# A two-layer decoder trunk: compressed-token products in four column groups of the matrix engine, a reordered way into the sparse head pairs, and the forget bias as bf16 pieces

## The chip, the core and the metric

The kernel runs on one core of a Trainium2 chip. The metric is the device time of one execution in microseconds, median of several. TensorE is called PE below, its weight loads PEld, VectorE DVE, ScalarE ACT, GpSimd POOL, and the engine that issues nearly all transfers SP.

## The reference, cut to what matters

Two layers on 256 tokens of width 2048, everything in f32. Layer 0 has 8 heads of sparse attention (compressed, selected and window branches) and 8 latent heads behind one input and one output projection. Layer 1 has 16 heads of forgetting attention. Each is followed by a SwiGLU network. Shift, scale and gate of every sub-layer come from a vector `c` through large matrices (`ada_w`, 6 x 2048 columns per layer), read whole and multiplied by `c`.

```python
def nsa_compress(k, pos_emb, w1, w2):      # blocks of 32 tokens, one every 16: 15 blocks
    blk = k[:, idx] + pos_emb[:, None, :]  # then flattened to CMP_LEN * d = 4096
    return jax.nn.silu(blk @ w1) @ w2      # w1 4096 x 256, for k and for v, two groups each
...
# forgetting attention: a bias per head, query and key on the logits
cum = lax.cumsum(jax.nn.log_sigmoid(f + f_b), axis=1)
logit = einsum(qq, k) * scale + cq[..., None] - cum[:, :, None, :]
```

## The kernel before, in words

One program per engine, with semaphores between them; nothing is scheduled at run time. The weights come through a ring of four 1 MB slots (`RAW`). SP issues the loads in one fixed order and waits, before each, until the slot four places back has been used. A slot holds one of three kinds of unit. A "w" unit is a block of a projection: ACT copies it rounded to `WHI`, DVE subtracts to get the rest `WLO` (two buffers each), and PE multiplies in three f32r products (L1129 to L1131). An "a" unit is 128 rows of `ada_w`: DVE multiplies it by a column of `c` and adds it to `ACC` (L1868 for the first, L1871 for the others), with no work for PE. An "r" unit is used by PE raw, in f32. An f32 product appears in the trace as two matmul instructions; an f32r or bf16 product as one.

**The passage to the sparse pairs.** The input projection of layer 0 runs as eight chunks, `even_in` 0 to 7; the last has 88 columns (gates and rotary key) and its result is kept as `GK`. After it come eight turns, one for each pair of sparse heads, p = 0 to 7. In a turn PE does `cmp_unit(p)` (L1411), which multiplies eight k-tiles of an r unit (`nsa_cmp_w1_k` for p below 4, `nsa_cmp_w1_v` above) by the blocks `BF` with 30 stationary columns; then `scores(p + 1)` (L1431), `values(p - 1)` (L1460 to L1463) and `turn_p(p)` (L1442, transposes of the softmaxed rows). DVE does `logits(p)` (L2159 to L2164), one a unit (L1871) and `outputs(p - 1)` (L2171 to L2184). ACT does `exps(p)` (L838) and the copy `turned(p)` (L848). SP loads one r unit and one a unit per turn.

Ahead of turn 0, DVE scales the latent rows (L2125), splits them into high and low parts (`CQH` by ACT, `CQL` by DVE, L1965), copies `GK` (L2099), does `logits(0)`, adds the four quarters of the gate vector from PE's column sums (`finish((0, G1))`, L1176 on PE and L1882 on DVE, through two PSUM banks), takes the gates from the turned `GK` (L2196, L2197), and only then builds `BF` (eight additions, L2206). `cmp_unit(0)` waits for them. ACT takes the sigmoid of the gates before `exps(0)`.

After turn 7 the sums in PSUM get their SiLU (L858), are turned (L1540), copied (L2230) and multiplied by `w2`, between the products of the latent heads.

**The forgetting attention.** Its input projection runs as 13 chunks and four more for the output gate. Eight of these 17 carry a head pair each: after their first unit PE does `fox_scores(p)`, for two heads and two row blocks: q times k in f32 (L1740), the key's forget bias (L1741, f32, 16 rows, the stationary operand a spread column of the identity that picks the head), and the causal mask (L1742, bf16). DVE turns the sums into `CUMT` once (L2608). PE turns two units later, and multiplies by the values three units later.

The causes of order are therefore the program texts of the five engines, the ring of four slots, and two buffers of `WHI`/`WLO`.

```python
def cmp_unit(n):
    ...
    ins = mm(m.PS[0:30, 0, 256 * i:256 * i + 256], m.BF[:, i, u.kt0 + k, :],
             m.RAW[:, u.s % RING, 256 * k:256 * k + 256], start=..., stop=...)
```

Of the kernel before, what the change touches and what calls it, by code (L numbers as in the profile page):

```python
# [23 lines left out]
KT = D // P  # L24
# [18 lines left out]
C_BLK, C_LEAD = 605, 609  # L43
C_ALL = 610
# [7 lines left out]
def constants():  # L52
# [14 lines left out]
    c[:, C_LEAD] = i % 32 == 0  # L67
    return c
# [122 lines left out]
class Machine:  # L191

    def __init__(self, nc, t, ctx, known):
# [20 lines left out]
        self.WLO = sb("WLO", [P, 2, 2048], F32R)  # L214

        ((self.AHI, self.ALO), (_, self.XG), (self.O, self.KN, self.RP, self.KRO, self.HCT, self.KCT, self.VCN), (_, self.BF)) = overlay(
# [3 lines left out]
             ("HCT", [P, 2, 2, 30], F32), ("KCT", [P, 32], F32), ("VCN", [P, 2, P], F32)],  # L220
            [("O_ROOM", [P, 16, T], F32), ("BF", [P, 2, 32, 30], F32)])
# [23 lines left out]
        self.NEGB = sb("NEGB", [P, P], BF16)  # L245
        self.VC = sb("VC", [P, V_ALL])
# [11 lines left out]
            [("Z", [P, 4, 2, 16], F32), ("CUM", [P, 2, 16], F32)])  # L258
# [15 lines left out]
        self.CUMT, self.FZ, self.FE, self.FL = (self.TF[0:16, i, :] for i in range(4))  # L274
        self.GK = self.TF[0:88, 0, :]
# [363 lines left out]
def scalar_program(block, nc, t, out, m):  # L639

    @block.scalar
    def _(act):
# [246 lines left out]
        hi(mla[1])  # L889
        mla_evict(0)  # L890
# [220 lines left out]
def tensor_program(block, nc, t, out, m):  # L1111

    @block.tensor
    def _(pe):
# [51 lines left out]
        def finish(v, blocks=range(KT)):  # L1166
# [3 lines left out]
            if v[1] in (G1, G2):  # L1170
                if v == (1, G1):
                    wait("t_read", ("fox", m.fox_at["k", 3]))
                for q in range(4):
# [232 lines left out]
        def cmp_unit(n):  # L1406
# [3 lines left out]
            for k in range(u.nk):  # L1410
                ins = mm(m.PS[0:30, 0, 256 * i:256 * i + 256], m.BF[:, i, u.kt0 + k, :], m.RAW[:, u.s % RING, 256 * k:256 * k + 256],  # L1411
                         start=u.kt0 + k == 0, stop=u.kt0 + k == 31)
# [123 lines left out]
        mla_unit(0)  # L1536
        for i in range(2):
            wait("st_copied", ("cmp", i))
# [4 lines left out]
        wait("t_read", ("cmp", 1))  # L1543
# [186 lines left out]
        def fox_scores(p):  # L1730
# [42 lines left out]
        def cumulate_turned():  # L1773

            wait("cum_ready", 0)
            for tb in range(2):
                ins = turn(m.PS[0:16, 5, P * tb:P * tb + P], m.CUM[:, tb, :], m.ID)
# [54 lines left out]
def vector_program(block, nc, t, out, m):  # L1832

    @block.vector
    def _(dve):
# [37 lines left out]
        def finish(v):  # L1873
# [3 lines left out]
            if seg in (G1, G2):  # L1877
                wait("grow_bias", 2 * layer + (seg == G2))
                for q in range(4):
# [113 lines left out]
        V.tensor_copy(m.IDB[:], m.ID)  # L1993
        link(V.tensor_copy(m.NEGB[:], m.CON[:, C_NEG:C_NEG + P]))
# [111 lines left out]
        def bias_masked():  # L2106
# [4 lines left out]
            link(ins)  # L2111

        def even_second(c):
# [8 lines left out]
            else:  # L2122
# [4 lines left out]
                split_lo(c.key, m.CQL[:, at:at + 4, :], m.TF[:], m.CQH[:, at:at + 4, :])  # L2127
# [88 lines left out]
        mla, mla_ada = [c.w[0] for c in m.mla_in], [[u for u in c.units if u.kind == "a"] for c in m.mla_in]  # L2216
        lo(mla[0])
# [11 lines left out]
        wait("t_done", ("cmp", 1))  # L2229
        m["t_read"].tick(V.tensor_copy(m.HCT[:].rearrange("p i j n -> p i (j n)"), m.PS[:, 6, 0:128].rearrange("p (i n) -> p i n", i=2)[:, :, 0:60]), ("cmp", 1))  # L2230
# [445 lines left out]
```

## Time and profile before

| | |
|---|---|
| median of 3 runs | 2571.3 us (2568.48 to 2573.88) |
| the profiled execution | 2571.42 us |
| its span in the trace | 2569.6 us |
| PE busy | 2480.1 us, 97% |
| DVE busy | 1708.0 us, 66% |
| ACT busy | 1028.9 us, 40% |
| mean granted clock of PE | 0.985 |
| moved by the transfers | 636.57 MB, mean 248 GB/s |

The span is what the trace covers; the 1.8 us beside it are the start and end of the execution. An engine's busy share is a mean over stages with different limits. "x" is a number of instructions, "<-" names what ended a wait. A clock of 1.00 is 2.4 GHz, 0.50 is 1.2 GHz.

### The profile page before, as it was taken

The numbers are of one execution on the slowest core, as the hardware profiler recorded it, in microseconds if no ns is written. First come the engines' busy times: TensorE is split into PE (matmuls) and PEld (weight loads), VectorE is DVE, ScalarE is ACT, GpSimd is POOL, SyncE is SP. The second block draws the span as 40 slices with busy tenths as digits, with TensorE's granted clock in tenths as the row PEclk, the third lists the DMA queues.
The fourth block names the chain that finished last, engine by engine and source line by source line (L and its number), as shares of the span: only waits on it lengthen the run. The fifth ranks groups of instructions, "written<-read, shape, count | busy, mean of one in ns | idle before, by whom it ended". The sixth has DMA issues, their size and how long they took to land.

```text
span 2569.6 us, 29279 instructions
## 1 busy us (share of the span) xinstructions
PE 2480.1 (97%) x11756; PEld 2011.1 (78%) x11756; DVE 1708.0 (66%) x1355; ACT 1028.9 (40%) x975; POOL 3.0 (0%) x9
## 2 busy tenths in 40 slices
PE   5899899999999999999999999999999999999998
PEld 3677577778878888888877888778788788888887
DVE  6878686886676767766766666668766554445446
ACT  2234344454333333343544444444543333333434
POOL 0000000000000000000000000000000000000000
PEclk8899999999999999999999999999999999999999
DMA  9989575868786877778788896889687655555553
GB/s 356 351 292 344 206 277 215 299 242 289 277 311 220 311 269 290 269 265 307 228 182 228 182 211 184 231 264 331 220 288 278 235 190 187 195 181 196 188 189 130
DMA packets 266196, 636.57 MB, mean 248 GB/s; under 512 B 15984, under 2 KB 26992, under 8 KB 244720
## 3 DMA queue, kind: packets, MB, share of 16 engines
q1 hardware_dynamic: 264800, 627.35, 73.7%
q0 software_dynamic: 720, 5.24, 0.6%
q10 hardware_dynamic: 576, 2.57, 0.2%
q8 instruction: 71, 1.16, 0.2%
q14 instruction: 29, 0.24, 0.0%
HBM read 633.03 MB, written 2.10 MB: 247 GB/s over the span
## 4 chain that ended last, share of the span: by engine, by line
PE 82%; DVE 8%; DMA 5%; ACT 3%; issue 2%; SPq 0%; DVEq 0%; ACTq 0%
PE PS L1129 23%; PE PS L1131 23%; PE PS L1130 23%; DVE WLO L1858 2%; ACT WHI L662 2%; DMA RAW<-in_fox_w_in 2%; DMA RAW<-in_even_w_in 1%; PE PS L1411 1%; DVE ACC L1871 1%; DMA PRO<-in_ada_w 1%; DVE ACC L1980 1%; PE PS L1431 1%; PE PS L1180 1%; PE PS L1697 1%; PE PS L1195 1%
## 5 line engine op out<-in xcount | busy, mean ns | idle before, releaser
L1129 PE MATMUL PS<-WHI,AHI 128*128 128x512 f32 x2024 | 796.3, 393 | 11.5 <-DVE WLO L1858 9.8
L1131 PE MATMUL PS<-WHI,ALO 128*128 128x512 f32 x2024 | 788.9, 390 | 0.0
L1130 PE MATMUL PS<-WLO,AHI 128*128 128x512 f32 x2024 | 788.4, 390 | 0.0
L1858 DVE TENSOR_TENSOR WLO<-RAW,WHI 128x2048 fp32r<-128x2048 f32 (+2 forms) x217 | 492.2, 2268 | 350.5 <-ACT WHI L662 350.2
L662 ACT ACTIVATE WHI<-RAW 128x2048 fp32r<-128x2048 f32 (+2 forms) x217 | 412.0, 1899 | 717.6 <-PE PS L1131 509.8
L2448 DVE TENSOR_TENSOR WLO<-RAW,WHI 128x2048 fp32r<-128x2048 f32 x174 | 398.8, 2292 | 351.6 <-ACT WHI L972 351.6
L972 ACT ACTIVATE WHI<-RAW 128x2048 fp32r<-128x2048 f32 x174 | 333.7, 1918 | 578.1 <-PE PS L1131 555.4
L1129 PEld LDWEIGHTS PS<-WHI,AHI 128*128 128x128 f32 x2024 | 380.4, 188 | 94.5 <-issue 7.1
L1131 PEld LDWEIGHTS PS<-WHI,ALO 128*128 128x128 f32 x2024 | 380.3, 188 | 80.3
L1130 PEld LDWEIGHTS PS<-WLO,AHI 128*128 128x128 f32 x2024 | 380.6, 188 | 76.7 <-issue 0.2
L1129 PE MATMUL PS<-WHI,GHI 128*128 128x512 f32 x864 | 340.9, 395 | 3.4 <-DVE WLO L1858 3.1
L1131 PE MATMUL PS<-WHI,GLO 128*128 128x512 f32 x864 | 337.0, 390 | 0.0
L1130 PE MATMUL PS<-WLO,GHI 128*128 128x512 f32 x864 | 336.7, 390 | 0.0
L1871 DVE SCALAR_TENSOR_TENSOR ACC<-RAW,COND,ACC 128x2048 f32<-128x2048 f32 x94 | 220.4, 2345 | 0.7
L1129 PEld LDWEIGHTS PS<-WHI,GHI 128*128 128x128 f32 x864 | 162.6, 188 | 40.2 <-issue 5.3
L1131 PEld LDWEIGHTS PS<-WHI,GLO 128*128 128x128 f32 x864 | 162.4, 188 | 34.2
L1130 PEld LDWEIGHTS PS<-WLO,GHI 128*128 128x128 f32 x864 | 162.7, 188 | 33.3 <-issue 0.5
L2459 DVE SCALAR_TENSOR_TENSOR ACC<-RAW,COND,ACC 128x2048 f32<-128x2048 f32 x60 | 140.7, 2345 | 0.1
L838 ACT ACTIVATE L<-L,NM 128x128 f32<-128x128 f32 x80 | 35.4, 446 | 62.4 <-DVE NM L2164 62.4
L1980 DVE SCALAR_TENSOR_TENSOR ACC<-PRO,COND,ACC 128x512 f32<-128x512 f32 x60 | 45.0, 750 | 6.9 <-DMA PRO<-in_ada_w 5.2
L1286 PE MATMUL PS<-WHI,AHI 128*128 128x512 f32 x96 | 41.5, 432 | 7.0 <-DVE ALO L1965 6.8
L2339 DVE TENSOR_TENSOR TF<-PS,GROW 128x1024 f32<-128x1024 f32 x28 | 34.2, 1221 | 14.7 <-PE PS L1131 14.7
(326 smaller groups left out, 1785.7 us busy)
## 6 DMA issues: line engine op xcount, KB each, us to landing
RAW<-in_ffn_w SPq DMA_DIRECT2D x264, 1024.0 KB, 5.2
RAW<-in_ada_w SPq DMA_DIRECT2D x176, 1024.0 KB, 5.9
RAW<-in_fox_w_in SPq DMA_DIRECT2D x64, 1024.0 KB, 8.2
RAW<-in_even_w_in SPq DMA_DIRECT2D x28, 1024.0 KB, 7.5
PRO<-in_ada_w SPq DMA_DIRECT2D x16, 1024.0 KB, 12.5
RAW<-in_even_w_out SPq DMA_DIRECT2D x16, 1024.0 KB, 7.3
RAW<-in_fox_w_out SPq DMA_DIRECT2D x16, 1024.0 KB, 6.7
GROW<-in_ada_b POOLq DMA_DIRECT2D x4, 1024.0 KB, 6.7
```

What stands on the lines that cost most here:

```text
L662: A(m.w_view(m.WHI, u), m.w_view(m.RAW, u), ACT.Copy).then_inc(m["hi_ready"].sem, 1)
L838: m["exp_done"].tick(A(m.L[:, b, h, cols], m.L[:, b, h, cols], ACT.Exp, bias=m.NM[:, b, j:j + 1], accum_out=m.SM[:, b, j:j + 1]), p)
L972: A(m.WHI[:, (up.w0 + j) % 2, :], m.RAW[:, (up.s0 + s) % RING, :], ACT.Copy).then_inc(m["hi_ready"].sem, 1)
L1129: mm(dst(tb), xh, whi[:, k, :], start=first and k == 0, stop=False)
L1130: mm(dst(tb), xh, wlo[:, k, :], start=False, stop=False)
L1131: ins = mm(dst(tb), xl, whi[:, k, :], start=False, stop=last and k == nk - 1)
L1286: mm(dst, xh, whi[:, k, :], start=kt == 0, stop=False)
L1858: TT(m.w_view(m.WLO, u), m.w_view(m.RAW, u), m.w_view(m.WHI, u).bitcast(F32), ALU.subtract).then_inc(m["lo_ready"].sem, 1)
L1871: STT(out=acc[:], in0=raw, scalar=m.COND[:, kt:kt + 1], in1=acc[:], op0=ALU.mult, op1=ALU.add).then_inc(m["ada_used"].sem, 1)
L1980: ins = STT(out=acc, in0=src, scalar=by, in1=acc, op0=ALU.mult, op1=ALU.add)
L2448: TT(m.WLO[:, (up.w0 + j) % 2, :], m.RAW[:, (up.s0 + s) % RING, :], m.WHI[:, (up.w0 + j) % 2, :].bitcast(F32), ALU.subtract).then_inc(m["l ...
L2459: STT(out=m.ACC[:], in0=m.RAW[:, slot, :], scalar=m.COND[:, col], in1=m.ACC[:], op0=ALU.mult, op1=ALU.add).then_inc(m["ada_used"].sem, 1)
```

## The change

`cmp_unit` spreads its k-tiles over four column groups of PE, so the sums lie in four bands of 32 partitions. The blocks `BF` get 32 columns (two of them zero) and lie in the second buffer of `WLO`; the first `lo` of the latent heads then waits for the last `cmp_unit`. ACT copies all four bands without SiLU, the turn of PE adds the bands (a product with a stacked identity of 128 rows), and ACT takes the SiLU from PSUM into `HCT`.

The passage is reordered. DVE builds `BF` before it copies `GK` and scales the last latent rows; two quarters of the gate vector are added before `logits(0)`, two after the gates; the low part `CQL` of the last latent rows comes after `logits(0)`. PE does `cmp_unit(0)` between the two halves of the column sums, and in each turn the order is `scores(p + 1)`, `values(p - 1)`, `cmp_unit(p + 1)`, `turn_p(p)`.

The forget bias of layer 1 is cut in three bf16 pieces. The sums of 16 heads are repeated six times over 96 columns; after the turn, DVE makes three bands of 32 rows (value rounded, rest rounded, rest of the rest) in `CUMB`, and the bias product becomes one bf16 product of 96 rows with `HEADB`. `CON` grows from 610 to 642 columns.

The tiles:

```diff
-            [("O_ROOM", [P, 16, T], F32), ("BF", [P, 2, 32, 30], F32)])
+            [("BF_ROOM", [P, 2048], F32), ("BF", [P, 2, 32, 32], F32)])
...
-        self.GK = self.TF[0:88, 0, :]
+        self.CUMB = self.TF[0:96, 0, 0:128].bitcast(BF16)
+        self.CUMV, self.CUMR = self.TF[0:96, 2, :], self.TF[0:96, 3, :]
+        self.GK = self.PT[0:88, 1, 0, 0:T]
```

On ACT, after turn 7:

```diff
-        for i in range(2):
-            act.wait_ge(m["row_used"].sem, m.cmp_in[i][-1].n + 1)
-            m["st_copied"].tick(A(m.ST[0:30, i, 0:256], m.PS[0:30, 0, 256 * i:256 * i + 256], ACT.Silu), ("cmp", i))
+        act.wait_ge(m["row_used"].sem, m.cmp_in[1][-1].n + 1)
+        m["st_copied"].tick(A(m.ST[:, :, 0:256], m.PS[:, 0, :].rearrange("p (i n) -> p i n", i=2), ACT.Copy), ("cmp", 1))
...
         hi(mla[1])
+        wait("t_done", ("cmp", 1))
+        m["cmp_h"].tick(A(m.HCT[:]..., m.PS[:, 6, 0:128]..., ACT.Silu), 0)
         mla_evict(0)
```

On PE:

```diff
             for k in range(u.nk):
-                ins = mm(m.PS[0:30, 0, 256 * i:256 * i + 256], m.BF[:, i, u.kt0 + k, :], ...,
-                         start=u.kt0 + k == 0, stop=u.kt0 + k == 31)
+                g = 32 * (k % 4)
+                ins = mm(m.PS[g:g + 32, 0, 256 * i:256 * i + 256], m.BF[:, i, u.kt0 + k, :], ...,
+                         start=u.kt0 + k < 4, stop=u.kt0 + k >= 28)
...
         scores(0)
-        finish((0, G1))
+        finish((0, G1), quarters=(0, 1))
         wait("gk_kept", ("even_in", 7))
+        wait("tf_ready", ("even_in", 6))
...
         wait("cmp_b", 0)
+        cmp_unit(0)
+        finish((0, G1), quarters=(2, 3))
+        wait("gates_in", ("even_in", 7))
         for p in range(8):
-            if p == 4:
-                wait("cmp_b", 1)
-            cmp_unit(p)
-            if p == 0:
-                wait("gates_in", ("even_in", 7))
-                wait("row_read", ((0, G1), 3))
             if p < 7:
                 scores(p + 1)
             if p:
                 values(p - 1)
+            if p == 3:
+                wait("cmp_b", 1)
+            if p < 7:
+                cmp_unit(p + 1)
+            if p == 0:
+                wait("row_read", ((0, G1), 3))
             turn_p(p)
...
-                ins = turn(m.PS[:, 6, 64 * i + 30 * j:64 * i + 30 * j + 30], m.ST[0:30, i, P * j:P * j + P], m.CON[0:30, C_ID:C_ID + 30])
+                ins = mm(m.PS[:, 6, 64 * i + 30 * j:64 * i + 30 * j + 30], m.ST[:, i, P * j:P * j + P], m.CON[:, C_STACK:C_STACK + 30], start=True, stop=True)
...
-                    mm(bank[:, at:at + n], m.CON[0:16, C_ID + h:C_ID + h + 1].to_broadcast([16, P]), m.CUMT[:, 0:n], start=False, stop=False)
+                    mm(bank[:, at:at + n], m.HEADB[0:96, h:h + 1].to_broadcast([96, P]), m.CUMB[:, 0:n], start=False, stop=False)
```

On DVE (`blocks` holds a memset and the eight additions of `BF`):

```diff
+            if c.i == 7:
+                blocks()
+                even_first(c)       # the copy of GK
...
+        finish((0, G1), (0, 1))
         logits(0)
-        finish((0, G1))
+        latent_low(m.even_in[6])
         wait("gk_turned", 0)
         ...
-        for i in range(2):
...
-                    ins = TT(m.BF[:, i, l0:l0 + 16, 15 * g:15 * g + 15], src, pos, ALU.add)
-                    m["cmp_b"].tick(ins, i)
+        finish((0, G1), (2, 3))
         for p in range(8):
...
+        dve.wait_ge(m["row_used"].sem, m.cmp_in[1][-1].n + 1)
         lo(mla[0])
...
-        m["t_read"].tick(V.tensor_copy(m.HCT[:]..., m.PS[:, 6, 0:128]...), ("cmp", 1))
...
-                m["cumt_ready"].tick(TS(m.CUMT, m.PS[0:16, 5, 0:256], -1.0 / FOX_SCALE, None, ALU.mult), 0)
+                link(TS(m.CUMV, m.PS[0:96, 5, 0:256], -1.0 / FOX_SCALE, None, ALU.mult))
+                link(V.tensor_copy(m.CUMB, m.CUMV))
+                link(TT(m.CUMR, m.CUMV, m.CUMB, ALU.subtract))
+                V.tensor_copy(m.CUMB[32:64], m.CUMR[32:64])
+                link(V.tensor_copy(m.CUMB[64:96], m.CUMR[64:96]))
+                link(TT(m.CUMR[64:96], m.CUMR[64:96], m.CUMB[64:96], ALU.subtract))
+                m["cumt_ready"].tick(V.tensor_copy(m.CUMB[64:96], m.CUMR[64:96]), 0)
```

## Rows read from the trace of the kernel before

**Rows 1.** Chain of waits: two compressed units that follow each other (start us, us, what).

```profile
308.60 3.57 PE PS L1411 x16
...
315.66 3.57 PE PS L1411 x16
```

**Rows 2.** Timeline of DVE: a unit of turn 1, one whole turn, the unit of turn 7.

```profile
288.90 2.35 DVE L1871 SCALAR_TENSOR_TENSOR ACC<-RAW,COND,ACC 128x2048 f32<-128x2048 f32 x1
...
309.09 0.95 DVE L2159 SCALAR_TENSOR_TENSOR L<-PS,BIAS 128x768 f32<-128x768 f32 x1
...
311.21 2.35 DVE L1871 SCALAR_TENSOR_TENSOR ACC<-RAW,COND,ACC 128x2048 f32<-128x2048 f32 x1
...
315.12 1.13 DVE L2182 TENSOR_SCALAR O<-PS,RC 128x128 f32<-128x128 f32 x4 [1.27 <-PE PS L1463]
...
332.40 2.35 DVE L1871 SCALAR_TENSOR_TENSOR ACC<-RAW,COND,ACC 128x2048 f32<-128x2048 f32 x1
```

**Rows 3.** Windows: busy us of each engine, granted clock, DMA share, GB/s.

```profile
260.00:270.00 10.00, 8.32 (x58) 6.91 (x56) 4.38 (x8) 2.34 (x2) 0.00 (x0) 1.00 0.54 194
270.00:280.00 10.00, 4.17 (x7) 1.72 (x8) 7.31 (x16) 1.94 (x5) 0.00 (x0) 0.66 0.00 0
...
310.00:320.00 10.00, 10.00 (x58) 6.53 (x56) 8.56 (x16) 4.28 (x16) 0.00 (x0) 1.00 0.86 313
```

**Rows 4.** Timeline of DVE from the last latent rows to turn 1.

```profile
265.33 1.66 DVE L2125 TENSOR_SCALAR TF<-PS,VC 128x256 f32<-128x256 f32 x4 [3.97 <-PE PS L1195]
268.53 1.23 DVE L1965 TENSOR_TENSOR CQL<-TF,CQH 128x1024 fp32r<-128x1024 f32 x1 [1.54 <-ACT CQH L673]
...
275.16 0.69 DVE L1882 TENSOR_TENSOR GROW<-PS,GROW 128x512 f32<-128x512 f32 x1 [1.57 <-PE PS L1176]
276.87 0.69 DVE L1882 TENSOR_TENSOR GROW<-PS,GROW 128x512 f32<-128x512 f32 x1 [1.02 <-PE PS L1176]
...
277.91 3.81 DVE L2206 TENSOR_TENSOR BF<-XT,VC 128x240 f32<-128x240 f32 x8
...
286.77 0.96 DVE L2159 SCALAR_TENSOR_TENSOR L<-PS,BIAS 128x768 f32<-128x768 f32 x1 [3.85 <-PE PS L1431]
```

**Rows 5.** Timeline of ACT between the sigmoid of the gates and the first exponentials.

```profile
278.29 1.28 ACT L838 ACT_TABLE_LOAD   x1
```

**Rows 6.** Timeline of PE, and L1350's weight loads: products already in four column groups.

```profile
88.62 1.06 PE L1350 MATMUL PS<-RAW,COND 128*32 128x512 f32 x8
...
L1350 PEld LDWEIGHTS PS<-RAW,COND x8: 105/106/108, 88.6 to 88.7; 128*32 128x32 f32 x8
```

**Rows 7.** Timeline of PE: scores of one forgetting pair, up to the next projection unit.

```profile
1382.77 0.38 PE L1740 MATMUL PS<-KT_F,QT_F 128*128 128x128 f32 x2
1383.08 0.48 PE L1741 MATMUL PS<-TF,CON 16*128 16x128 f32 x2
1383.49 0.23 PE L1742 MATMUL PS<-NEGB,IDB 128*128 128x128 bf16 x1
1383.56 0.65 PE L1740 MATMUL PS<-KT_F,QT_F 128*128 128x256 f32 x2
1384.14 0.69 PE L1741 MATMUL PS<-TF,CON 16*128 16x256 f32 x2
1384.77 0.23 PE L1742 MATMUL PS<-NEGB,IDB 128*128 128x128 bf16 x1
...
1386.93 0.48 PE L1129 MATMUL PS<-WHI,AHI 128*128 128x512 f32 x1
```

**Rows 8.** Waits, 1370 to 1700 us: us in total, times, longest.

```profile
PEld PS L1741 <- issue: 5.3, 16, 0.3
```

**Rows 9.** Timeline of DVE: the old conversion of the forget bias.

```profile
1377.38 0.41 DVE L2608 TENSOR_SCALAR TF<-PS 16x256 f32<-16x256 f32 x1 [0.32 <-PE PS L1777]
```

**Rows 10.** A window in the forgetting projection, and the chain at its end.

```profile
1460.00:1490.00 30.00, 30.00 (x144) 24.00 (x143) 17.66 (x18) 13.94 (x18) 0.00 (x0) 1.00 0.98 192
...
1687.35 11.14 DMA RAW<-in_fox_w_in
```

More of the change, by code:

```diff
@@ L213, in __init__ @@
         self.WHI = sb("WHI", [P, 2, 2048], F32R)
-        self.WLO = sb("WLO", [P, 2, 2048], F32R)
-        ((self.AHI, self.ALO), (_, self.XG), (self.O, self.KN, self.RP, self.KRO, self.HCT, self.KCT, self.VCN), (_, self.BF)) = overlay(
+        (self.WLO,), (_, self.BF) = overlay(
+            [("WLO", [P, 2, 2048], F32R)],
+            [("BF_ROOM", [P, 2048], F32), ("BF", [P, 2, 32, 32], F32)])
+        ((self.AHI, self.ALO), (_, self.XG), (self.O, self.KN, self.RP, self.KRO, self.HCT, self.KCT, self.VCN)) = overlay(
             [("AHI", [P, KT, T], F32R), ("ALO", [P, KT, T], F32R)],
@@ L273, in __init__ @@
         self.PART = self.RS[:, 2, 4:6]
-        self.CUMT, self.FZ, self.FE, self.FL = (self.TF[0:16, i, :] for i in range(4))
-        self.GK = self.TF[0:88, 0, :]
+        self.FZ, self.FE, self.FL = (self.TF[0:16, i, :] for i in range(1, 4))
+        self.CUMB = self.TF[0:96, 0, 0:128].bitcast(BF16)
+        self.CUMV, self.CUMR = self.TF[0:96, 2, :], self.TF[0:96, 3, :]
+        self.GK = self.PT[0:88, 1, 0, 0:T]
         self.RB, self.RBS, self.GB, self.FB = (self.VC[:, a:b] for a, b in ((V_RB, V_RBS), (V_RBS, V_GB), (V_GB, V_FB), (V_FB, V_ALL)))
@@ L496, in t_freed_by @@
             return ("lo_split", key)
+        if key == ("cmp", 1):
+            return ("cmp_h", 0)
         return ("t_read", key)
@@ L889, in _ @@
         hi(mla[1])
+        wait("t_done", ("cmp", 1))
+        m["cmp_h"].tick(A(m.HCT[:].rearrange("p i j n -> p i (j n)"), m.PS[:, 6, 0:128].rearrange("p (i n) -> p i n", i=2)[:, :, 0:60], ACT.Silu), 0)
         mla_evict(0)
@@ L1164, in unit, with finish @@
             ins.then_inc(m["w_used"].sem, 1)
-        def finish(v, blocks=range(KT)):
+        def finish(v, blocks=range(KT), quarters=range(4)):
             pe.wait_ge(m["ada_used"].sem, ADA_DONE[v])
@@ L1172, in finish @@
                     wait("t_read", ("fox", m.fox_at["k", 3]))
-                for q in range(4):
+                for q in quarters:
                     if q >= 2:
@@ L1776, in cumulate_turned @@
             for tb in range(2):
-                ins = turn(m.PS[0:16, 5, P * tb:P * tb + P], m.CUM[:, tb, :], m.ID)
+                ins = turn(m.PS[0:96, 5, P * tb:P * tb + P], m.CUM[:, tb].rearrange("p r h -> p (r h)"), m.ID)
             m["cumt_done"].tick(ins, 0)
@@ L1871, in ada, with finish @@
                 STT(out=acc[:], in0=raw, scalar=m.COND[:, kt:kt + 1], in1=acc[:], op0=ALU.mult, op1=ALU.add).then_inc(m["ada_used"].sem, 1)
-        def finish(v):
+        def finish(v, quarters=range(4)):
             layer, seg = v
@@ L1878, in finish @@
                 wait("grow_bias", 2 * layer + (seg == G2))
-                for q in range(4):
+                for q in quarters:
                     wait("ada_sum", (v, q))
@@ L2111, in bias_masked, with blocks, latent_low @@
             link(ins)
+        def blocks():
+            link(V.memset(m.BF[:, :, :, 30:32], 0.0))
+            for i in range(2):
+                at = (V_PK, V_PV)[i]
+                for g in range(2):
+                    for half in range(2):
+                        l0 = 16 * half
+                        src = m.XT[:, 8 + 2 * i + g, l0:l0 + 240].rearrange("p (n l) -> p l n", l=16)
+                        pos = m.VC[:, at + l0:at + l0 + 16].unsqueeze(2).to_broadcast([P, 16, 15])
+                        ins = TT(m.BF[:, i, l0:l0 + 16, 15 * g:15 * g + 15], src, pos, ALU.add)
+                        m["cmp_b"].tick(ins, i)
+        def latent_low(c):
+            at = 4 * (c.i - 5)
+            split_lo(c.key, m.CQL[:, at:at + 4, :], m.TF[:], m.CQH[:, at:at + 4, :])
         def even_second(c):
@@ L2126, in even_second @@
                 dve.wait_ge(m["tf_ready"].sem, m["tf_ready"].value)
-                split_lo(c.key, m.CQL[:, at:at + 4, :], m.TF[:], m.CQH[:, at:at + 4, :])
+                if c.i == 5:
+                    latent_low(c)
         def even_between(c, j):
@@ L2135, in even_between @@
                 angles()
-        run(m.even_in[3:], even_first, even_second, between=even_between)
+            if c.i == 7:
+                blocks()
+                even_first(c)
+        run(m.even_in[3:], even_first, even_second, between=even_between, last=lambda c: None)
         def logits(p):
```

30 lines of the change are left out of this document (12 added, 18 removed).

## The prediction

> **What bounds the kernel now.** I read the chain that ended last first: almost all of it is PE. The change touches two stretches, the passage to the sparse pairs with its eight turns (about 260 to 340 us) and the forgetting projection (about 1370 to 1700 us), so each is read by its own rows.
>
> In the turns, one compressed unit follows the other after 7.06 us and is itself 3.57 us of that [rows 1]. PE is busy 10.00 of 10 us there at clock 1.00, while the transfers have a share of 0.86 and move 313 GB/s [rows 3]. DVE in one turn does its logits from 309.09, its unit from 311.21, waits 1.27 us for PE's values, and does the outputs from 315.12 [rows 2]. So PE bounds a turn of 7.07 us, and DVE, with 7.07 - 1.27 = 5.80 us, is next. The turns from the unit of turn 1 (288.90) to that of turn 7 (332.40) take 43.5 us, six of them [rows 2].
>
> Ahead of the turns nobody is the bound: between 270 and 280 us PE is busy 4.17 of 10 us, the transfers move nothing (the ring is full and no slot comes free), and the clock is 0.66 on the mean [rows 3]. It is a relay between DVE, PE and ACT. DVE waits 3.97 us before it scales the latent rows, 1.54 for ACT's high part, 1.57 and 1.02 for column sums, builds the blocks for 3.81 us, and waits 3.85 us for the scores that PE puts behind its first compressed unit [rows 4].
>
> In the forgetting projection PE is busy 30.00 of 30 us at clock 1.00 [rows 10]. One pair's scores last from 1382.77 to 1386.93, 4.16 us [rows 7], and there are eight pairs.
>
> **The change part by part.**
>
> *Compressed units.* The nearest rows are products that already lie in four column groups: eight instructions of 512 columns take 1.06 us [rows 6]. A new unit has sixteen instructions of 256 columns, the same columns, so I take 1.1 us; the bounds are 1.0 and the present 3.57. PE's turn becomes 7.07 - 3.57 + 1.1 = 4.6 us and stops being the bound. What is late next is DVE with 5.80 us, and beside it the transfers: 313 GB/s at share 0.86 [rows 3] is 364 GB/s at full share, and the 2.10 MB of a turn need 2.10 / 364 = 5.8 us. Two limits so close do not mesh perfectly; I take 5.9 us (bounds 5.8 and 6.6; 6.6 is what the transfers would take if they stayed at some 318 GB/s). The ring can carry it: a slot is taken again two turns, 11.8 us, after its last use. The bound on PE's side would be reached only by a unit of 2.4 us. Six turns give 43.5 - 6 x 5.9 = **8.1 us**.
>
> DVE's last wait in a turn, 1.27 us for PE's values [rows 2], goes: the values no longer stand behind a unit of 3.57 us [rows 1], and DVE asks only 1.27 us sooner.
>
> For the column groups the Trainium skill, page "TensorE: Matmul & The Clock Gate", section "Part 3: Packing small matmuls — row/col tiling", has a rule that speaks against them: weight loads overlap running matmuls only when the row groups differ, and here all four groups use all rows. Here the row differs: eight loads start within 0.1 us and the whole lasts 1.06 us [rows 6]. What the sum would be by the rule stands among the rivals.
>
> *The way in.* The eight additions (3.81 us) move into DVE's wait of 3.97 us; with the memset in front, which no row shows (0.2 us; bounds 0.1 and the 0.69 of an addition of 512 columns [rows 4]), and the copy of `GK` (0.4 us, as the like one in [rows 9]), which now goes first, the scaling of the latent rows starts some 0.7 us later. Then `CQL` no longer waits (1.54 us), since `logits(0)` lies between; the column sums are ready when DVE asks (1.57 + 1.02 us), and so are the scores (3.85 us), which no longer queue behind a compressed unit. Sum: 3.81 + 1.54 + 1.57 + 1.02 + 3.85 - 0.7 = **11.1 us**, by which the unit of turn 1 starts earlier, at about 277.8 (bounds 8 and 12). The scarcest cover is ACT's: after the gates it has the sigmoid, the table load of 1.28 us [rows 5] and the exponentials, and then come turn, copy and values. By my count the values of pair 0 come just as DVE wants them at full clock, and about 2 us late if PE is at half clock; the lower bound takes that in. The transfers start again at about 270 instead of 285. In the old order the low clock follows PE's idle stretch [rows 3]; the new order leaves fewer such holes, and I count nothing for it.
>
> New waits: PE's `tf_ready` before the turn of `GK` has scores and two column sums ahead of it, about as long; behind it stand the turn and the first compressed unit. PE's wait for a compressed load now stands ahead of `turn_p`, so a late load also delays ACT's copy; the loads are two turns ahead. DVE's wait before `lo(mla[0])` is for a unit done one turn earlier: free.
>
> *Behind the turns.* ACT's copy saves a table load there, and has the SiLU and its load behind `hi(mla[1])`, where it waits for a transfer anyway; DVE loses a short copy. Zero, bounds -0.5 and 1. The transfers, full to the end of the turns, hand the latent heads a fuller queue: I take **-1.0 us** (0 to -3).
>
> *Forget bias.* The two f32 instructions go from 1383.08 to 1383.49 (128 columns, 0.41) and from 1384.14 to 1384.77 (256 columns, 0.63) [rows 7], twice per pair: 2.08 us. One bf16 product of 128 columns goes from 1383.49 to 1383.56, 0.07 us [rows 7], so one of 256 takes about 0.12, and the new ones are 0.38 us. Also, PE pauses about 0.1 us on each side of the 16-row products: its sequencer shows waits of its own, 5.3 us in 16 [rows 8], while the 128-row bf16 mask between f32 products has none; that is 0.4 us per pair ahead of L1741, gone if 96 rows count as a full product. So 2.08 - 0.38 + 0.4 = 2.1 us per pair, 16.9 us in eight (bounds: without the pauses' end, on both sides, 0.95 x 8 = 7.6; and 17.5).
>
> The Trainium skill, page "TensorEngine Tiling (Array Packing)", "Key Properties", says that changing the tiling mode drains the engine; by its modes 96 rows are a product without row tiling. The pauses at the 16-row products agree; that 96 rows have none, no row here shows.
>
> Not all of it stays. In the slow part of the projection the transfers are at share 0.98 with 192 GB/s [rows 10], little behind PE, and at its end a transfer of 11.14 us is on the chain [rows 10]. I take off the last pair's 2.1 us, whose stretch runs into that transfer, and 0.5 for the rest: **14.3 us**. The longer conversion on DVE, seven instructions of about 0.4 [rows 9] instead of one, is 2.4 us more, and PE needs it only at 1383.08 [rows 7], 5.7 us after the old one began [rows 9]: hidden behind a projection unit, zero; without that cover 2.4 us, once. The wider copy, the broadcast and the larger constant table are 0.2 us beside others.
>
> **Sum.** 8.1 + 11.1 - 1.0 + 14.3 = 32.5 us off the profiled execution's own 2571.42 us (its span is 2569.6; the median shown, 2571.3, is the same within 0.1): 2571.4 - 32.5 = **2539 us**. The runs shown span 5 us, 0.2%, about what a measurement of this kernel can tell from no change.
>
> **The rivals.**
>
> *The pauses stay with 96 rows, or the bf16 pieces cost nearly what the f32 product did.* The forget part gives 7.6 - 2.6 = 5 us: 2571.4 - (18.2 + 5) = 2548. For it: no row has 96 rows. Against it: the mask's row. Chance 0.13.
>
> *Transfers end last in both stretches.* Turns of 6.6 us give 3.9 us instead of 8.1, and in the forgetting projection the three pairs in the slow part give nothing more, 6.3 us: 2539 + 4.2 + 6.3 = 2549. For it: share 0.98 [rows 10]. Against it: PE never waits within that window. Chance 0.13.
>
> *The loads of the column groups come one after another.* As a mechanism here: 16 loads of 0.105 us [rows 6] stand beside four rounds of 0.21, so a unit is 2.6 us, PE's turn 6.1, and six turns are 1.2 us dearer: 2540. If nothing overlaps at all, a unit stays at 3.57, the 8.1 us are lost and also some 2 of the way in: 2549. By the skill's rule it would be the first; the row speaks against both. Chance 0.07 together.
>
> *Slower: PE sinks to half clock.* With idle holes in each turn (1.3 us of 5.9) the clock may fall in the turns and behind them. Where PE is the bound, a stretch at half clock takes twice its time. From 32 us of gain, it needs 32 us of PE's work at the low level beyond the present to cancel, about half of all that PE does in the turns; above that the kernel is slower, 2580 if it lasts through turns and latent heads. Against it: with PE busy 8.32 of 10 us the clock stayed 1.00, and it was low where PE was busy 4.17 of 10 [rows 3]. Chance 0.03.
>
> *The change does not reach the chain:* gains swallowed, 2571. Chance 0.02.
>
> **How the numbers follow.** My forecast has chance 0.62; its own range is 2531 to 2546. The predicted time is 2539. The range goes down to 2530 (all upper bounds: 10 + 12 + 17) and up to 2552, to take in the first three rivals. Faster by over 0.2%: 0.95. Within 0.2%: 0.02. Slower: 0.03.
>
> **What would show it.** Right: compressed units of about 1.1 us; 5.8 to 6.0 us from one unit of `ACC` to the next, with DVE nearly without waits and transfers above 0.95; the unit of turn 1 near 278; a pair's scores of 2.1 us and no sequencer wait at the bias product; clock 1.00 in the turns. Wrong: turns over 6.4 us with PE or DVE waiting on transfers; scores of 3 us or more; new PE waits for `WLO` in the forgetting projection; more windows at half clock.

## The result, and the profile after

| | before | after |
|---|---|---|
| median | 2569.9 us (4 runs, 2567.2 to 2573.9) | 2532.9 us (4 runs, 2530.9 to 2535.2) |
| ratio | | 0.9855, 95% interval 0.9838 to 0.9872 |
| span of the profiled execution | 2569.6 us | 2530.3 us |
| mean granted clock of PE | 0.985 | 0.985 |

The forecast was 2539 us with a range of 2530 to 2552. The change is worth 37 us by the medians and 39.3 us by the two spans, where the forecast had 32.5. One of nine executions of the kernel before that ran beside e1 to e4 took 14082 us; the ratios below leave it out.

**The turns.** DVE's timeline after the change, from the blocks of the compressed products to the unit of turn 2, and the unit of turn 7:

```profile
260.94 3.95 DVE L2136 TENSOR_TENSOR BF<-XT,VC 128x240 f32<-128x240 f32 x8
...
270.52 1.22 DVE L1978 TENSOR_TENSOR CQL<-TF,CQH 128x1024 fp32r<-128x1024 f32 x1
...
276.60 2.35 DVE L1884 SCALAR_TENSOR_TENSOR ACC<-RAW,COND,ACC 128x2048 f32<-128x2048 f32 x1
...
282.44 2.35 DVE L1884 SCALAR_TENSOR_TENSOR ACC<-RAW,COND,ACC 128x2048 f32<-128x2048 f32 x1
...
311.58 2.35 DVE L1884 SCALAR_TENSOR_TENSOR ACC<-RAW,COND,ACC 128x2048 f32<-128x2048 f32 x1
```

No line ends in a bracket: between 260 and 285 us DVE waits for nobody, where [rows 4] had five waits. From the unit of turn 1 to that of turn 7 it is 35.0 us, 5.83 a turn. The same stretch in windows (PE, PEld, DVE, ACT, POOL busy; clock, DMA share, GB/s) answers to [rows 3]:

```profile
260.00:270.00 10.00, 10.00 (x73) 7.61 (x72) 9.70 (x21) 2.34 (x2) 0.00 (x0) 1.00 0.52 176
270.00:280.00 10.00, 7.64 (x68) 5.19 (x66) 9.79 (x18) 5.95 (x19) 0.00 (x0) 1.00 0.77 254
280.00:290.00 10.00, 8.74 (x84) 7.38 (x84) 9.79 (x18) 5.11 (x17) 0.00 (x0) 1.00 1.03 361
290.00:300.00 10.00, 8.31 (x79) 6.88 (x68) 9.72 (x23) 3.73 (x12) 0.00 (x0) 1.00 1.05 373
```

DVE is now the full column (9.7 to 9.8 of 10), PE has holes, the transfers stand at share 1.03 to 1.05, and the clock of the way in is 1.00 instead of 0.66. PE's timeline shows the new unit, and one that waits for its load:

```profile
273.61 1.07 PE L1420 MATMUL PS<-RAW,BF 128*32 128x256 f32 x16
...
295.61 1.07 PE L1420 MATMUL PS<-RAW,BF 128*32 128x256 f32 x16 [1.69 <-DMA RAW<-in_nsa_cmp_w_v]
```

A unit lasts 1.07 us instead of 3.57 [rows 1]. The wait in brackets costs nothing as long as DVE keeps its 5.83 us.

**The forgetting pairs.** PE's timeline over the first half of a pair's scores, and the end of the block, which answers to [rows 7]:

```profile
1364.71 0.38 PE L1753 MATMUL PS<-KT_F,QT_F 128*128 128x128 f32 x2
1364.93 0.22 PE L1754 MATMUL PS<-TF,HEADB 96*128 96x128 bf16 x1
1364.99 0.22 PE L1755 MATMUL PS<-NEGB,IDB 128*128 128x128 bf16 x1
1365.05 0.65 PE L1753 MATMUL PS<-KT_F,QT_F 128*128 128x256 f32 x2
1365.54 0.27 PE L1754 MATMUL PS<-TF,HEADB 96*128 96x256 bf16 x1
1365.65 0.22 PE L1755 MATMUL PS<-NEGB,IDB 128*128 128x128 bf16 x1
...
1366.73 0.48 PE L1137 MATMUL PS<-WHI,AHI 128*128 128x512 f32 x1
```

From 1364.71 to 1366.73 it is 2.02 us instead of 4.16. (Durations overlap; what an instruction costs is the distance of the starts: 0.06 and 0.11 us for the two bias products.) The trace has no sequencer wait at L1754 or L1755, where [rows 8] had 5.3 us in 16 at the bias product. The same view of the kernel before has a second such row, at the mask that stands right behind that product:

```profile
PEld PS L1742 <- issue: 5.3, 16, 0.3
```

It is gone as well.

**Where the time went, by stage.** The same DVE instruction in both traces, after minus before, read at the ends of the stages:

| stage (us of before) | forecast | measured |
|---|---|---|
| ahead of the change, to 257 | 0 | -0.7 |
| way in, to the unit of turn 1 | -11.1 | -11.6 |
| turns 1 to 7 | -8.1 | -8.5 |
| behind them, to 1375 | +1.0 | +0.3 |
| entry to the first pair, to 1385 | 0 | +2.5 |
| eight pairs | -16.9, with the last 2.6 lost again | -17.2 |
| end of the forgetting projection, to 1712 | | -3.8 |
| to the end | 0 | -0.3 |

A minus is time won. The measured column adds up to the 39.3 us of the spans, the forecast column with the 2.6 us lost again to 32.5.

### The profile page after: what moved, and what is told of

Read it like the earlier page. It is cut to its first block, busy times and chain, and to the rows that moved or that the text cites. A ratio compares the mean times of both kernels' runs of the same rounds, so it can differ in the third digit from the quotient of the medians.

```text
span 2530.3 us, 29231 instructions
## 1 busy us (share of the span) xinstructions
PE 2445.4 (97%) x11728; PEld 2002.3 (79%) x11728; DVE 1709.2 (68%) x1362; ACT 1027.9 (41%) x975; POOL 3.0 (0%) x9
## 4 chain that ended last, share of the span: by engine, by line
PE 82%; DVE 8%; DMA 5%; ACT 2%; issue 2%; SPq 0%; ACTq 0%; DVEq 0%
PE PS L1137 24%; PE PS L1139 24%; PE PS L1138 24%; DVE WLO L1871 2%; ACT WHI L669 2%; DMA RAW<-in_fox_w_in 2%; DVE ACC L1884 1%; DMA PRO<-in_ada_w 1%; DVE ACC L1993 1%; PE PS L1188 1%; PE PS L1710 1%; PE PS L1203 1%; DMA RAW<-in_ada_w 1%; PE PS L1294 1%; DMA RAW<-in_even_w_in 1%
```

## The experiments

Each kernel is the changed one with one edit, and "against the change" means against its trace. e1 to e4 ran on one chip, e5, e6, e7 and e9 on one, and e8 and e10 to e12 on one, each time with the kernel before beside them.

**e1: the f32 bias product with 16 rows again.**

```diff
-mm(..., m.HEADB[0:96, h:h + 1].to_broadcast([96, P]), m.CUMB[:, 0:n], ...)
+mm(..., m.CON[0:16, C_ID + h:C_ID + h + 1].to_broadcast([16, P]), m.CUMV[0:16, 0:n], ...)
```

and on DVE the one conversion of before in place of the seven. Expected:

> The changed kernel with the forget bias as before (one f32 product of 16 rows, one conversion on DVE), all else kept. Theory (each part acts by itself, PE bounds the projection): a pair's scores take 4.16 us again instead of 2.01, and with eight pairs the kernel is 8 x 2.15 = 17.2 us slower than the changed one, about 2550 us, 20 us faster than the kernel before. Rival (the bias is worth less than its eight blocks, since the transfers swallow part of it, and the rest of the gain behind the first layer is the luck of the clock): 10 to 14 us slower than the changed kernel, about 2545.

Measured: 2551.2 us (2548.6 to 2557.7), ratio to before 0.9931 (0.9905 to 0.9957); a pair's scores 4.16 us, and both wait rows of before are back:

```profile
PEld PS L1755 <- issue: 5.3, 16, 0.3
PEld PS L1754 <- issue: 5.3, 16, 0.3
```

The span is 18.2 us longer than the change's; eight times 2.15 is 17.2. Read at the same DVE instructions from the first pair's entry to behind the last pair, the change wins 17.2 us on the kernel before and e1 none. So the forgetting part is worth that, and hardly anything of it is swallowed by the transfers.

**e2: one column group instead of four.**

```diff
-g = 32 * (k % 4)
+g = 32 * (k % 1)
```

with the start and stop flags, and the copy and fold of 32 rows, to match. Expected:

> The changed kernel with all compressed products in one column group, order and all else kept. Theory (column groups make the turns short): a unit takes 3.57 us again, a turn 7.07 us with PE as the bound, so six turns are 7.5 us longer, and the first unit on the way in 1 to 2.5 us: 9 to 10 us slower than the changed kernel, about 2542. Rival (the new order, with the values ahead of the unit, is what shortens the turns): turns of 6 us and 3 us or less lost, about 2535.

Measured: 2541.6 us (2540.0 to 2546.2), ratio 0.9891 (0.9868 to 0.9913). PE's and DVE's timelines of this kernel:

```profile
287.12 3.64 PE L1420 MATMUL PS<-RAW,BF 128*32 128x256 f32 x16
...
294.15 3.64 PE L1420 MATMUL PS<-RAW,BF 128*32 128x256 f32 x16
```

```profile
275.92 2.35 DVE L1884 SCALAR_TENSOR_TENSOR ACC<-RAW,COND,ACC 128x2048 f32<-128x2048 f32 x1
```

With units of 3.64 us PE bounds the turn at 7.03 us again. But the unit of turn 1 stands at 275.92, as early as with the groups: the new order alone shortens the way in, by 10.9 us (13.0 at that unit against before, of which 2.1 were there ahead of the change). The first unit therefore costs 0.7 us on the way in, not the 1 to 2.5 expected.

**e3: the four groups with the order, the bias and the conversion of before.** The groups and the fold stay; `scores(0)`, `finish`, `GK`, the blocks and `cmp_unit(p)` stand where they stood before. Expected:

> The kernel before with the column groups alone: old order, old place of the blocks, old forget bias. Theory: a unit takes 1.07 us, turns 5.8 us with DVE as the bound (-7.5 us), the first unit 3 to 4 us less than 5.33, so 11 to 12 us faster than the kernel before, ratio 0.9955; the way in keeps its waits. Rival (groups pay only with the new order): PE or DVE waits in the turns, turns of 6.4 us or more, 7 us or less.

Measured: 2559.7 us (2557.8 to 2562.4), ratio 0.9961 (0.9946 to 0.9975). Window and DVE's timeline:

```profile
270.00:280.00 10.00, 5.54 (x22) 2.23 (x22) 7.31 (x17) 3.39 (x10) 0.00 (x0) 0.50 0.00 0
```

```profile
285.49 2.35 DVE L1876 SCALAR_TENSOR_TENSOR ACC<-RAW,COND,ACC 128x2048 f32<-128x2048 f32 x1
...
320.47 2.35 DVE L1876 SCALAR_TENSOR_TENSOR ACC<-RAW,COND,ACC 128x2048 f32<-128x2048 f32 x1
```

The turns are 5.83 us: these are the groups' own 8.5 us. On the way in the transfers stand still and the clock is low as before, and the groups bring 1.8 us there (3.4 less 1.6 from ahead), where 3 to 4 were expected. So the two parts overlap by only 2 us: 1.8 + 8.5 = 10.3 from the groups and 10.9 + 0.9 = 11.8 from the order (e2's turns against those of before), 22.1 in all, against 11.6 + 8.5 = 20.1 together. Behind the turns this kernel gives back 4 us and wins 3.8 us at the end of the forgetting projection, a place that is taken up below.

**e4: two column groups** (`32 * (k % 2)`), a unit between the two. Expected:

> The changed kernel with two column groups instead of four (bands of 64 rows are read). Theory (PE has room in the turns): a unit takes about 2.0 us, PE's turn is 5.5 us, still under DVE's 5.8, so the turns stay at 5.8 us and the time is that of the changed kernel, within 1 us (the first unit may cost 0.9). Rival (PE still sets the turn, as it waits for loads and then for ACT): turns of 6.5 us or more, 5 us slower.

Measured: 2537.6 us (2536.4 to 2539.2), ratio 0.987 (0.9852 to 0.9888). The unit lasts 1.92 us, the turns stay at 5.83 us:

```profile
290.42 1.92 PE L1420 MATMUL PS<-RAW,BF 128*32 128x256 f32 x16
```

```profile
289.01 2.35 DVE L1884 SCALAR_TENSOR_TENSOR ACC<-RAW,COND,ACC 128x2048 f32<-128x2048 f32 x1
294.85 2.35 DVE L1884 SCALAR_TENSOR_TENSOR ACC<-RAW,COND,ACC 128x2048 f32<-128x2048 f32 x1
```

So a unit of 1.92 us serves the turn as well as one of 1.07, as the prediction's bound of 2.4 us says, and the third and fourth group buy nothing there; nor on the way in, which is 11.6 us shorter than before, as with four. Yet the median is 4.7 us above the change's, where 1 was expected. By itself that shows nothing: the change run again, e12, has 2536.2 us, and its ratio to the kernel before beside it, 0.9871, is that of e4. The trace shows where this execution lost its time. It runs 2.3 us behind the change's at 1639 us and 6.6 us behind at 1681. In between, in code that the edit does not touch, PE waits once for DVE, which waits for a load (the row of waits, and two windows):

```profile
PE PS L1137 <- DVE WLO L1871: 3.2, 1, 3.2
```

```profile
1668.00:1673.00 5.00, 2.50 (x7) 2.07 (x8) 4.66 (x3) 2.85 (x3) 0.00 (x0) 0.81 0.80 257
1673.00:1678.00 5.00, 5.00 (x20) 4.04 (x20) 3.33 (x2) 0.11 (x1) 0.00 (x0) 0.85 1.01 302
```

PE is busy 2.50 of 5 us, and behind the hole the clock is 0.81 and 0.85. The kernel before has the same hole at the same unit; the change has none (below).

**e5 and e6: what of the bias product costs.** Two edits of one line that split the 2.15 us a pair. e5 keeps bf16 but gives it 16 rows (it leaves out the second and third piece of the bias):

```diff
-mm(..., m.HEADB[0:96, h:h + 1].to_broadcast([96, P]), m.CUMB[:, 0:n], ...)
+mm(..., m.HEADB[0:16, h:h + 1].to_broadcast([16, P]), m.CUMB[0:16, 0:n], ...)
```

> Leaves out the second and third bf16 piece of the forget bias: the two bf16 bias products have 16 rows and the first piece only. Theory (PE pauses beside a product of few rows): the sequencer's waits come back at the bias product, about 0.1 us on each side of it, so a pair's scores last 2.01 + 0.4 to 0.8 = 2.4 to 2.8 us, and the kernel loses 3 to 6 us against the change. Rival (the pauses belonged to the switch between f32 and bf16 data): scores stay at 2.0 us and no waits appear.

e6 keeps 96 rows but f32 (`m.CON[0:96, C_ID + h:C_ID + h + 1]` and `m.CUMV[:, 0:n]`; the column of the identity takes the head's own row alone, so the whole bias is added after all):

> The bias products stay f32 but have 96 rows (the kept pieces, one of 32 columns of an identity as weights; the numbers are other ones than the reference's). Theory: no sequencer waits, scores of 4.16 less 0.4 to 0.8 = 3.4 to 3.8 us a pair against the 2.01 of the change and the 4.16 of before, so the bf16 data themselves are worth 1.4 to 1.8 us a pair and the full product of rows the rest. Rival (pauses belong to the f32 data): scores stay at 4.16 us with waits.

Measured, each in one execution: 2536.3 and 2544.6 us; the scores of every one of the eight pairs 2.83 us in e5 and 2.99 us in e6. PE's timelines, e5 and then e6, and the wait row of e5:

```profile
1362.24 0.38 PE L1753 MATMUL PS<-KT_F,QT_F 128*128 128x128 f32 x2
1362.56 0.22 PE L1754 MATMUL PS<-TF,HEADB 16*128 16x128 bf16 x1
1362.71 0.23 PE L1755 MATMUL PS<-NEGB,IDB 128*128 128x128 bf16 x1
```

```profile
1368.39 0.38 PE L1753 MATMUL PS<-KT_F,QT_F 128*128 128x128 f32 x2
1368.61 0.39 PE L1754 MATMUL PS<-TF,CON 96*128 96x128 f32 x2
1368.83 0.22 PE L1755 MATMUL PS<-NEGB,IDB 128*128 128x128 bf16 x1
```

```profile
PEld PS L1754 <- issue: 5.3, 16, 0.3
```

Only the rows differ between e5 and the change, and the waits are back, 0.1 us on each side of a product (0.32 instead of 0.22 ahead of it, 0.15 instead of 0.06 behind), 0.82 us a pair, just above what I expected. e6 has no such row: f32 data alone bring no pause, and the rival falls in both. Of the 2.15 us the 96 rows are 4.16 - 2.99 = 1.17 and bf16 is 2.99 - 2.01 = 0.98. I had expected 3.4 to 3.8 for e6: the pauses of an f32 product of 16 rows are about 0.3 us, not 0.1 to 0.2. An f32 product is two instructions. From its start to the mask it takes 0.41 us with 16 rows [rows 7] and 0.22 with 96, so it has a third pause of 0.1 us, between its own two instructions. The prediction had most of them hidden in the durations that it took from [rows 7] (0.41 us for a product that is 0.22 us with 96 rows), and so its sum was right. The two totals say little about the scores: ahead of the change's stretch e5 already ran 2.2 us before the change, and e6 1.7 us behind it.

**e7, e9, e10: what bounds the new turn.** e7 lets DVE add only half the columns of the gain sums in the turns, e9 loads only half the columns of those units (the other half is stale), e10 does both; each leaves that part of the sums out.

```diff
-STT(out=acc[:], in0=raw, scalar=m.COND[:, kt:kt + 1], in1=acc[:], ...)
+cols = slice(0, 1024) if u in m.nsa_ada else slice(0, 2048)
+STT(out=acc[:, cols], in0=raw[:, cols], scalar=m.COND[:, kt:kt + 1], in1=acc[:, cols], ...)
...
+if u in m.nsa_ada:
+    sp.dma_start(m.RAW[:, slot, 0:1024], t["ada_w"][layer][P * kt:P * kt + P, D * seg:D * seg + 1024]).then_inc(full, 16)
+    return
```

> Leaves out half of the columns of the gain sums that DVE adds in the turns. Theory (DVE is the bound of a turn with 5.83 us, the transfers right behind with about 5.7): DVE is some 1.1 us shorter, but the turns get only to 5.6 to 5.8 us, and DVE shows waits for transfers. Rival (only DVE matters, the ring gives what is asked): turns of 4.7 us, 6.5 us less over six of them.

> The units that DVE adds in the turns are loaded over half of their columns only (the other half is stale). A turn then loads 1.57 MB instead of 2.10. Theory (DVE bounds the turn): turns stay at 5.83 us within 0.1, and PE's waits for compressed loads go. Rival (the transfers bound it, DVE merely follows): turns shorten towards 4.7 us, or at least under 5.6.

> Leaves out half of the columns of the gain sums in the turns, both from DVE's additions and from the loads. With DVE's part alone cut the turns took 5.26 us and DVE waited for transfers; with the loads alone cut they stayed at 5.83. Theory (DVE's own 5.83 less 1.07 = 4.76 us is the bound once the transfers have 1.57 MB a turn): turns of 4.8 to 4.9 us without waits for transfers. Rival (the wait for PE's values, of 0.3 to 0.5 us, is the next bound, not the transfers): turns stay at 5.2 to 5.3.

Measured, one execution each: 2528.5, 2536.4 and 2525.6 us. DVE's timelines, e9 (turns 5.83), e7 and e10:

```profile
291.02 2.35 DVE L1887 SCALAR_TENSOR_TENSOR ACC<-RAW,COND,ACC 128x2048 f32<-128x2048 f32 x1
296.85 2.35 DVE L1887 SCALAR_TENSOR_TENSOR ACC<-RAW,COND,ACC 128x2048 f32<-128x2048 f32 x1
```

```profile
286.30 1.28 DVE L1885 SCALAR_TENSOR_TENSOR ACC<-RAW,COND,ACC 128x1024 f32<-128x1024 f32 x1
...
291.57 1.28 DVE L1885 SCALAR_TENSOR_TENSOR ACC<-RAW,COND,ACC 128x1024 f32<-128x1024 f32 x1 [0.42 <-DMA RAW<-in_ada_w]
...
296.95 1.28 DVE L1885 SCALAR_TENSOR_TENSOR ACC<-RAW,COND,ACC 128x1024 f32<-128x1024 f32 x1 [0.26 <-DMA RAW<-in_ada_w]
...
302.57 1.28 DVE L1885 SCALAR_TENSOR_TENSOR ACC<-RAW,COND,ACC 128x1024 f32<-128x1024 f32 x1 [0.28 <-DMA RAW<-in_ada_w]
```

```profile
291.81 1.28 DVE L1888 SCALAR_TENSOR_TENSOR ACC<-RAW,COND,ACC 128x1024 f32<-128x1024 f32 x1
...
296.58 1.28 DVE L1888 SCALAR_TENSOR_TENSOR ACC<-RAW,COND,ACC 128x1024 f32<-128x1024 f32 x1
```

With a quarter of the loads gone the turn does not move (e9), and PE's waits for compressed loads are gone: DVE bounds it. With 1.07 us less on DVE the last four turns, in each of which DVE waits for a load, take 5.27 to 5.62 us, 5.4 on the mean (e7). The turn ahead of them waits for none and takes 4.77; the 5.26 us that stands in e10's expectation is a mean with this turn in it, and is too low for the transfers' limit. With both cut five of the six turns take 4.77 us, DVE's own 5.83 - 1.07, and no load is waited for (e10). In both kernels the first of the six takes 5.81 us, with a wait of 1.1 us for PE's values, so that turn would gain nothing from a lighter DVE. For the others the order of the limits is DVE 5.83, transfers 5.4, DVE's remaining work 4.77. My expectation for e7, 5.6 to 5.8, had the transfers somewhat too slow: in that kernel they moved 389 GB/s between 280 and 290 us instead of the 361 of the change, because DVE, not they, had set that figure.

```profile
280.00:290.00 10.00, 8.44 (x81) 6.76 (x80) 9.69 (x24) 5.34 (x18) 0.00 (x0) 1.00 1.06 389
```

**e8, e11, e12: two versions on DVE's path, and the change again.** In e8 `latent_low(m.even_in[6])` goes from ahead of the turns to behind `lo(mla[1])`. e11 also does the outputs of the selected pairs in one product:

```diff
-for j in range(4): ... TS(o, ps[:, P * j:P * j + P], by, None, ALU.mult)
+TT(m.O[:, h0:h0 + 2, :].rearrange("p h (b d) -> p (h b) d", b=2), ps.rearrange("p (a d) -> p a d", a=4),
+   m.RC[:, b, :].unsqueeze(2).to_broadcast([P, 4, P]), ALU.mult)
```

> A version to better the change: DVE's low part of the latent rows (1.22 us) goes from between the gates and the first turn to behind the turns, after the low part of the second latent unit. Theory: the way in is DVE's own work, so the unit of turn 1 starts 1.2 us earlier (at 275.4 from 276.6) and the kernel ends 1 us earlier, below what a measurement can tell. Rival (the low part is then late for the latent heads, which wait for transfers anyway): the 1.2 us come back behind the turns.

> The same, and the outputs of the four pairs of selected blocks by one product of 512 columns instead of four of 128 columns. Four take 1.12 us; an addition of 512 columns takes 0.68 us. Theory (DVE bounds those turns at 5.83, the transfers only at 5.26): four turns of 5.4 us, so 1.8 us more, 3 us in all against the change. Rival (nothing, since the wait for PE's values grows by as much): turns of 5.83 and 1.2 us in all.

> The changed kernel once more, beside the two versions. Every theory: 2530 to 2536 us, the same time as before within 0.1%, turns of 5.83 us, scores of 2.01 us.

| | median us (range, 4 runs each) | ratio to before | span |
|---|---|---|---|
| e12, the change | 2536.2 (2531.8 to 2536.8) | 0.9871 (0.9855 to 0.9888) | 2529.8 |
| e8 | 2531.2 (2529.4 to 2538.8) | 0.9859 (0.9837 to 0.988) | 2529.0 |
| e11 | 2530.5 (2526.8 to 2534.2) | 0.9853 (0.9837 to 0.987) | 2525.0 |

DVE's timeline of e11:

```profile
281.40 2.35 DVE L1884 SCALAR_TENSOR_TENSOR ACC<-RAW,COND,ACC 128x2048 f32<-128x2048 f32 x1
286.80 2.35 DVE L1884 SCALAR_TENSOR_TENSOR ACC<-RAW,COND,ACC 128x2048 f32<-128x2048 f32 x1
...
297.60 2.35 DVE L1884 SCALAR_TENSOR_TENSOR ACC<-RAW,COND,ACC 128x2048 f32<-128x2048 f32 x1
303.42 2.35 DVE L1884 SCALAR_TENSOR_TENSOR ACC<-RAW,COND,ACC 128x2048 f32<-128x2048 f32 x1
```

The four shortened turns take 5.40 us and the others 5.82, as the theory has it. From ahead of the way in to the unit of turn 7 e11 wins 2.9 us on the change, against 3 expected, and e8 1.15 us up to the unit of turn 1, against 1.2; behind the turns nothing of it comes back. The medians of e11 and e12 are 5.6 us apart, but the intervals overlap: that e11 is faster is shown by its turns, and by the medians only as likely. e12's median is 3.3 us (0.13%) above the first one of the same kernel, just outside the 0.1% expected, which says how far 4 runs carry.

## Why the prediction was right, point by point

The forecast was 6.8 us short of the 39.3 won by the spans. Nearly all of that is one place, the end of the forgetting projection (2.6 us that were not lost, 3.8 that were won). The other stages are off by up to 0.7 us in the change's favour and by 2.5 us against it at the entry to the pairs, and cancel to 0.4. The time lies near the lower end of the range. That end, 2530, is lower than its own sum: 10 + 12 + 17 give 2532, and the turns' bound of 5.8 us gives 8.7 and not 10, so 2534. Among the rivals, the 32 us of PE's work in "slower" are not half of what PE does in the new turns but most of it (8 times 4.6 is 37).

**Compressed unit.** Forecast 1.1 us, 1.07 measured. The Trainium skill's rule ("TensorE: Matmul & The Clock Gate", "Part 3: Packing small matmuls — row/col tiling"), that weight loads overlap only when the row groups differ, does not hold here: with one group a unit is 3.64 us, with two 1.92, with four 1.07, and all four use all rows. Sixteen weight loads of 0.11 us, 1.8 us one after another, fit in a unit of 1.07. That rival is out.

**The turn.** Forecast 5.9 us with DVE first and the transfers right behind; 5.83 measured, DVE without waits. e9 and e10 show the bound. The transfers' own limit, which I put at 5.8 from a full share, is about 5.4 (e7); the term came out because DVE was the larger.

**The way in.** Forecast 11.1, measured 11.6, all five waits gone. e2 shows that the order alone brings 10.9, so it was right to keep it apart from the groups. What each of its moves wins was not measured one by one. That the clock would rise there too (0.66 to 1.00) I had counted for nothing. The blocks cost 3.95 us instead of 3.81, the memset 0.17.

**Forget bias, per pair.** Forecast 2.1, measured 2.15, and no sequencer wait at the product of 96 rows, which no row of before could show. One premise was misread: the mask between f32 products was said to have no wait, but the trace of before has the same 5.3 us in 16 there (L1742 above). The wait belonged to the 16-row product ahead of the mask: it is gone in the change and in e6, where the mask is the same. The lower bound of 7.6 us was also too low, since bf16 with its pauses (e5) still gives 4.16 - 2.83 = 1.33 us a pair, 10.6 in eight. The Trainium skill's rule ("TensorEngine Tiling (Array Packing)", "Key Properties"), a drain where the tiling mode changes, agrees with the pauses on the two sides of a 16-row product and with their absence in e6. It does not account for the third one, between the two 16-row instructions of one f32 product, where the mode stays; the cause of the pauses is open. The longer conversion is 2.6 us and hidden, as said.

**The end of the forgetting projection: the step that failed.** I took off 2.1 us for the last pair and 0.5 beside it, because a load of 11.14 us stood on the chain there [rows 10]. Nothing was lost; 3.8 us more were won. In the kernel before, PE waits 2.70 us for `WLO` at that place, and runs at the low clock behind it:

```profile
1700.00:1705.00 5.00, 2.30 (x9) 1.72 (x9) 4.25 (x2) 3.25 (x3) 0.00 (x0) 0.93 0.88 283
1705.00:1710.00 5.00, 5.00 (x18) 4.01 (x17) 3.73 (x3) 0.00 (x0) 0.00 (x0) 0.73 1.01 305
```

In the change, at the same units, 38 us earlier:

```profile
1662.00:1667.00 5.00, 5.00 (x23) 3.88 (x22) 3.29 (x2) 1.98 (x2) 0.00 (x0) 1.00 0.98 306
1667.00:1672.00 5.00, 5.00 (x24) 4.12 (x23) 4.47 (x3) 2.15 (x3) 0.00 (x0) 1.00 1.05 352
```

Of the change and the eleven kernels made from it or from before, only e4 has the hole (e12 has not either), and e1 and e3, whose bias is that of before, have not. So it does not come from the bias product. The load that ends it takes 11.1 us from issue to landing in the kernel before and 11.7 in e4, but 8.5 in the change and in e12 and 9.1 in e1 and e3. Why it is slower in two kernels is open. It is the place where e4 lost 4.3 of its 6.6 us, and 3.8 of the 39.3 us come from it and from none of the terms of the sum.

**Behind the turns, and the entry to the pairs.** I had 1.0 us given back; it was 0.3. At the entry to the first pair 2.5 us more were given back, where the clock fell behind a wait of PE of 2.7 us:

```profile
1345.00:1350.00 5.00, 2.95 (x21) 2.57 (x19) 1.71 (x1) 1.91 (x1) 0.00 (x0) 0.99 1.01 402
1350.00:1355.00 5.00, 4.36 (x10) 3.47 (x11) 5.00 (x5) 1.91 (x1) 0.00 (x0) 0.50 1.06 366
```

In the second trace of the same kernel, e12, the wait was 1.4 us, and the same 5 us had the clock at 1.00, with PE busy 3.58 of them:

```profile
1350.00:1355.00 5.00, 3.58 (x22) 3.02 (x20) 5.00 (x4) 1.76 (x1) 0.00 (x0) 1.00 1.06 384
```

So this varies between executions of one kernel. Nor is it the new conversion of the bias, which starts only at 1359.44. But the length of the wait does not decide it: e1 and e11 wait 2.7 and 2.8 us there and keep the clock at 1.00. Why the clock falls in one and not in the other is open. That the change makes it more frequent is not excluded: e1 and e3, with the bias of before, give nothing back there, and most of the others 1 to 2.7 us. The latent heads vary likewise: e12 is 2.05 us later than the change between 336 and 352 us, which is most of the 2.7 us that e4 lost there. Two such places with 2 to 4 us each are what the 6 us between the fastest and slowest run of one kernel can be made of; I have not tied any one run to one of them.

**The rivals.** Pauses that stay: out by the block of 2.02 us, though not by the mask's row, which had been misread. Transfers that end last: out in the turns by e9; in the forgetting projection by e1, which gives back all of it. Slower by the clock: PE is busy 7.6 to 8.7 of 10 us in the turns up to 300 us, and 7.0 in the next 10, and the clock is 1.00. The clock did fall behind them (0.66 between 315 and 320 us), but the whole stage from turn 7 to 1375 us is only 0.3 us longer than before.

## What to carry to other kernels

Cost an edit in the stage's own chain and ask for the next engine's turn time: the cut of 2.5 us in PE's unit was worth 1.24 us a turn, because DVE stood there, and a cut to 1.92 would have done the same. To order the limits of such a loop, cut each suspect to half by itself and then both. And a product with few rows between full ones costs more than its columns: the pauses sit in the neighbours' distances, so read the starts over the whole block, not the one instruction.

## What the runs showed of the hardware

- A product of 16 rows between products of 128 rows costs about 0.2 us more than one of 96 rows in bf16 (2.83 against 2.01 us for a block with four of them) and about 0.3 us more in f32 (4.16 against 2.99), where its two instructions also pause between each other; with 96 rows there is no pause.
- Sixteen products of 256 columns with 32 output rows take 3.64, 1.92 and 1.07 us in one, two and four column groups, though each needs another 128-row weight load of 0.11 us.
- The transfers moved 383 to 391 GB/s at share 1.05 to 1.06 in the turns of e7, against 361 to 373 at 1.01 to 1.05 in the change, where DVE freed the slots later; a share of over 1 was not yet the limit.
- Behind waits of PE of the same length at the same place (2.7 us) the granted clock fell to 0.50 in the change's trace and stayed at 1.00 in e1's.
